# A fused transformer layer on one core: the first expert product's order, its biases, and how the last norm's rows are loaded

## The reference

```python
h = hybrid_mixer(x, ...);            x = layer_norm(ALPHA * x + h, ln1_g, ln1_b)
h = memory_cross_attention(x, ...);  x = layer_norm(ALPHA * x + h, ln2_g, ln2_b)
logits = x @ w_router + b_router     # top 4 of 32, softmax over the four
h = x @ w_gate_up[e] + b_gate_up[e]  # for each chosen expert e: 1024 -> 2048
g, u = h[:, :1024], h[:, 1024:]
g = minimum(g, 7);  u = clip(u, -7, 7)
y = ((u + 1) * g * sigmoid(1.702 * g)) @ w_down[e] + b_down[e]
x = layer_norm(ALPHA * x + sum of gate * y, ln3_g, ln3_b)
```

## Time and profile before

| | |
|---|---|
| median of 3 runs | 1207.15 us (1206.78 to 1207.22) |
| profiled execution, its own time | 1207.5 us |
| span of that profile | 1205.6 us |
| granted TensorE clock, mean | 0.995 |
| busy in the span: PE, PEld, DVE, ACT, POOL | 1148.1, 521.5, 221.0, 132.7, 49.7 us |
| DMA traffic | 446.63 MB, mean 370 GB/s |
| chain that ended last | PE 61%, DMA 35%, DVE 2% |

### The profile page before, as it was taken

How to read it: one execution, slowest core, us unless ns; L and a number is a source line. 1 busy time by engine, 2 the same in 40 slices (tenths; PEclk the granted TensorE clock), 3 DMA queues, 4 the chain that set the end, 5 groups by cost and what they waited for, 6 DMA issues and landing times.

```text
span 1205.6 us, 12958 instructions
## 1 busy us (share of the span) xinstructions
PE 1148.1 (95%) x5354; PEld 521.5 (43%) x5354; DVE 221.0 (18%) x560; ACT 132.7 (11%) x280; POOL 49.7 (4%) x56
## 2 busy tenths in 40 slices
PE   9999999999999999999999999898989899999986
PEld 7686746754434343433333443333333333333322
DVE  1233112224211111121111111111111111111114
ACT  2133102221100000001000000000000000000001
POOL 0232003010000000000000000000000000000001
PEclk9999999999999999999999999999999999999998
DMA  9953333397999999999999999999999999999995
GB/s 351 315 209 140 138 120 132 134 354 301 430 426 428 427 427 425 429 430 427 427 430 427 427 427 429 428 429 428 428 428 429 428 428 429 429 428 428 429 427 210
DMA packets 55411, 446.63 MB, mean 370 GB/s; under 512 B 10273, under 2 KB 11441, under 8 KB 30161
## 3 DMA queue, kind: packets, MB, share of 16 engines
q1 hardware_dynamic: 52912, 439.96, 87.9%
q10 hardware_dynamic: 2464, 6.18, 1.4%
HBM read 445.06 MB, written 1.07 MB: 370 GB/s over the span
## 4 chain that ended last, share of the span: by engine, by line
PE 61%; DMA 35%; DVE 2%; issue 1%; ACT 0%; SPq 0%
DMA ring<-in_w_gate_up 32%; PE bank L1673 22%; PE bank L1317 9%; PE bank L1698 9%; PE bank L1304 8%; DMA ring<-in_w_down 3%; PE bank L1557 3%; PE bank L1618 2%; PE bank L1633 1%; PE bank L1338 1%; PE bank L1744 1%; PE bank L1687 1%; PE bank L1502 1%; PE bank L1480 1%; DMA ring<-in_w_in 1%
## 5 line engine op out<-in xcount | busy, mean ns | idle before, releaser
L1673 PE MATMUL bank<-ring,PT 128*64 128x512 f32 x1848 | 409.2, 594 | 30.2 <-DMA ring<-in_w_gate_up 30.2
L1673 PEld LDWEIGHTS bank<-ring,PT 128*64 128x64 f32 x1848 | 129.7, 137 | 303.6 <-issue 242.4
L1166 DVE TENSOR_SCALAR reg_k<-bank 128x512 f32<-128x512 f32 x32 | 22.1, 692 | 455.0 <-PE bank L1673 455.0
L1304 PE MATMUL bank<-reg_bc,ring 128*128 128x256 f32 x448 | 99.7, 381 | 1.8 <-ACT reg_bc L717 1.8
L786 ACT ACTIVATE reg_v<-reg_k 128x512 f32<-128x512 f32 x30 | 18.9, 630 | 690.7 <-DVE reg_k L1166 690.7
L1698 PE MATMUL bank<-reg_q,NCt 128*64 128x512 f32 x400 | 92.5, 605 | 0.0
L1304 PEld LDWEIGHTS bank<-reg_bc,ring 128*128 128x128 f32 x448 | 84.2, 190 | 15.8 <-issue 4.8
L1698 PE MATMUL bank<-reg_bc,NCt 128*64 128x512 f32 x400 | 90.1, 592 | 0.0
L1557 PEld LDWEIGHTS bank<-L,reg_a 128*128 128x128 f32 x512 | 62.9, 196 | 24.8 <-issue 23.5
L1557 PE MATMUL bank<-L,reg_a 128*128 128x128 f32 x512 | 69.3, 288 | 1.0 <-DVE L L1080 0.7
L1197 DVE COPY reg_v<-bank 128x512 f32<-128x512 f32 x28 | 19.4, 692 | 269.0 <-PE bank L1698 269.0
(11 more groups left out here) (230 smaller groups left out, 693.1 us busy)
## 6 DMA issues: line engine op xcount, KB each, us to landing
ring<-in_w_gate_up SPq DMA_DIRECT2D x115, 2048.0 KB, 23.6
reg_bc<-in_w_down SPq DMA_DIRECT2D x26, 2048.0 KB, 20.7
reg_q<-in_w_down SPq DMA_DIRECT2D x25, 2048.0 KB, 19.2
ring<-in_w_down SPq DMA_DIRECT2D x9, 2048.0 KB, 19.0
ring<-in_w_in SPq DMA_DIRECT2D x5, 2048.0 KB, 17.7
reg_kv<-in_w_gate_up SPq DMA_DIRECT2D x5, 2048.0 KB, 18.5
reg_q<-in_w_gate_up SPq DMA_DIRECT2D x4, 2048.0 KB, 14.8
ring<-in_w_down SPq DMA_DIRECT2D x7, 1024.0 KB, 7.8
```

Of the source, the lines that this page charges most:

```text
L1166: nc.vector.tensor_scalar(gbuf, banks[0][:, :], LIMIT, None, ALU.min).then_inc(g_ready, 1)
L1304: last = mm(B(name)[:, a * T:(a + 1) * T], w[:, k, c:c + P], src[:, k, :], start=(k == 0), stop=(k == KD - 1))
L1673: last = mm(ps[half * CAP:(half + 1) * CAP, :], xgT[:, k, i * CAP:(i + 1) * CAP], w[:, j, col:col + HALF], start=False, stop=(k == KD - 1) ...
```

## The change

Five edits. (1) The first gate/up product has a function of its own, `first_gate_up`, that takes `k` in the order 1, 2, 3, 0, 4, 5, 6, 7; the lent half is thus fourth. (2) Its biases are added inside it ahead of `k` = 6, and not ahead of the rank product; in their old place stands the first tile's part of the rank. (3) Load 11 is now issued by halves like 9 and 10. (4) VectorE's order for the second tile: one copy of transposes goes to ScalarE, `gain2(0)` comes ahead, `scaled(1)` behind `rpart_copy(1)`. (5) `ln3_g` and `ln3_b` are loaded as single rows into partition 0; in the last pair TensorE multiplies a one-row matrix of ones with them (`spread_ln3`), and ScalarE copies the four results back to `x_nat`. The core of the diff:

```diff
             sp.wait_ge(opened, 2)
             load_half(NSLOT + 1, 0, ahead2_in)
-            wait_opening(1)
+            sp.wait_ge(opened, 3)
             load_half(NSLOT + 1, 1, slot_in[1])
-            for n in range(NSLOT + 2, OPEN * 2 * CH):
+            sp.wait_ge(opened, 4)
+            load_half(NSLOT + 2, 0, ahead3_in)
+            wait_opening(2)
+            load_half(NSLOT + 2, 1, slot_in[2])
+            for n in range(NSLOT + 3, OPEN * 2 * CH):
...
             copy(("rT", 1, 0), rT[:, 0:4, :], four(("rT", 1, 0)))
+            copy(("rT", 1, 1), rT[:, 4:8, :], four(("rT", 1, 1)))
             std(1, 1)
...
-            load_ln(2, ln3_g, ln3_b)
+            act.dma_start(x_nat[0:1, 0, :], ln3_g).then_inc(ln_in[2], 16)
+            act.dma_start(x_nat[0:1, 1, :], ln3_b).then_inc(ln_in[2], 16)
...
             pair(NE // 2 - 1, last=True)
+            for r in range(2):
+                act.wait_ge(ln3_rows, r + 1)
+                for half, ps in enumerate((gate_ps, up_ps)):
+                    nc.scalar.activation(x_nat[:, r, half * HALF:(half + 1) * HALF], ps[:, :], ACT.Copy).then_inc(ln3_spread, 1)
...
             variance(1, 1)
-            rT_copy(1)
-            scaled(1)
-            rpart_copy(1)
...
             dve.wait_ge(ln_in[1], 32)
+            dve.wait_ge(var_ready, TT + 2)
             gain2(0)
+            rpart_copy(1)
+            scaled(1)
             logits(1)
...
+            def rank_of_first_tile():
+                wait_bank(pe, ("rank", 1))
+                mm(B(("rank", 1))[:, 0:NE], one, M[:, 0, :], start=True, stop=False)
...
+            def first_gate_up():
+
+                pe.wait_ge(xgTa_sb, 1)
+                for n, k in enumerate((1, 2, 3, 0, 4, 5, 6, 7)):
+                    if k == 4:
+                        pe.wait_ge(xgTb_sb, 1)
+                    c, j = k // GUJ, k % GUJ
+                    if k == 0:
+                        pe.wait_ge(lent_in, 16)
+                        w = lent
+                    else:
+                        w = chunk(0, 0, c, "open")
+                    if k == 6:
+                        pe.wait_ge(bgu_in, 64)
+                        biases(0, 0, opens=False)
+                    for ps, c0 in zip((gate_ps, up_ps), (0, F)):
+                        for half in range(2):
+                            col = c0 + half * HALF
+                            last = mm(ps[half * CAP:(half + 1) * CAP, :], xgT[:, k, 0:CAP],
+                                      w[:, j, col:col + HALF], start=(n == 0), stop=(k == KD - 1), skip_group_check=True)
+                    if k in (1, 2, 3, 4):
+                        last.then_inc(opened, 1)
+                    elif k == 0:
+                        last.then_inc(chunks_used, 2)
+                    elif k == 5:
+                        last.then_inc(chunks_used, 1)
                 last.then_inc(gu_done, 1)
...
-                gate_up(0, 0, "open")
+                first_gate_up()
...
+            def spread_ln3(r):
+                if r == 0:
+                    pe.wait_ge(ln_in[2], 32)
+                    pe.wait_ge(gu_read, NE)
+                else:
+                    pe.wait_ge(ln3_spread, 2)
+                for half, ps in enumerate((gate_ps, up_ps)):
+                    last = mm(ps[:, :], one[0:1, :], x_nat[0:1, r, half * HALF:(half + 1) * HALF], start=True, stop=True)
+                last.then_inc(ln3_rows, 1)
...
-                final_down(p, 0, xy_ps, hT, lambda: transpose_h(p * 2 + 2))
+                final_down(p, 0, xy_ps, hT, second_result)
+                spread_ln3(1)
...
-            pe.wait_ge(bgu_in, 64)
-            biases(0, 0)
+            rank_of_first_tile()
             rank(1)
```

More of the change, by code:

```diff
@@ L1541, in router @@
                 fill(mm(B(name)[:, 0:NE], rsb[:, tt, :], K[:, C_STK:C_STK + NE], start=True, stop=True), name)
+            def rank_of_first_tile():
+                wait_bank(pe, ("rank", 1))
+                mm(B(("rank", 1))[:, 0:NE], one, M[:, 0, :], start=True, stop=False)
             def rank(tt):
                 name = ("rank", tt)
[L1545 to L1547 removed]
+                if tt == 0:
+                    wait_bank(pe, name)
                 pe.wait_ge(mask_ready, tt + 1)
@@ L1624, in scattered, with biases @@
                     pass
-            def biases(n, i, banks=(gate_ps, up_ps)):
+            def biases(n, i, banks=(gate_ps, up_ps), opens=True):
                 if not (type(n) is int and n < 2):
@@ L1632, in biases @@
                     rows = slice(g * 2 * NE, (g + 1) * 2 * NE)
-                    mm(ps[:, :], bsel[rows, i, :], bgu[rows, :], start=True, stop=False, skip_group_check=True)
+                    mm(ps[:, :], bsel[rows, i, :], bgu[rows, :], start=opens, stop=False, skip_group_check=True)
             def chunk(p, i, c, stage):
@@ L1659, in gate_up @@
                     pe.wait_ge(xgTa_sb, p + 1)
-                opening = stage == "open" and type(p) is int and p == 0
-                for n, k in enumerate([1, 0] + list(range(2, KD)) if opening and i == 0 else range(KD)):
+                for k in range(KD):
                     if i == 0 and k == KD // 2:
@@ L1664, in gate_up @@
                     c, j = k // GUJ, k % GUJ
-                    if n % GUJ == 0:
+                    if j == 0:
                         w = chunk(p, i, c, stage)
-                    if opening and (i, k) == (0, 0):
-                        pe.wait_ge(lent_in, 16)
-                        w = lent
                     for ps, c0 in zip(banks, (0, F)):
@@ L1674, in gate_up @@
                                       w[:, j, col:col + HALF], start=False, stop=(k == KD - 1), skip_group_check=True)
-                    if opening and (i, n) in ((0, 0), (0, 2)):
-                        last.then_inc(opened, 1)
-                    elif n % GUJ == GUJ - 1 and k < KD - 1:
+                    if j == GUJ - 1 and k < KD - 1:
                         last.then_inc(chunks_used, 1)
@@ L1680, in gate_up @@
                             behind[c]()
+                last.then_inc(gu_done, 1)
+            def first_gate_up():
[23 more added lines that the diff above has]
+                        last.then_inc(chunks_used, 1)
                 last.then_inc(gu_done, 1)
```

23 lines of the change are left out of this document (14 added, 9 removed).

## The result

The changed kernel takes **1212.95 us** (median of 5 runs, 1212.56 to 1213.87) against 1207.22 (1206.78 to 1208.47) for the kernel before: ratio 1.0047, 95% interval 1.0036 to 1.0059. It is 5.7 us slower; the prediction was 1208.0, range 1206.0 to 1209.9, so it was wrong. The profiled execution takes 1212.95 with a span of 1211.1, 5.5 more than before.

What follows compares the result with a forecast made beforehand. From about 300 us an unbroken expert-weight stream was taken to set the end, except the opening and last 25 us. Start 0, stream -2.1, spreading +2.9 gave +0.8 us: 1208.3 profiled, 1208.0 median, range 1206.0 to 1209.9.

Steps and rivals of the forecast that it cites:

- The start, 286.82, I hold fixed: Start of the first gate/up product: unchanged, net 0, between -0.2 and +0.3 us, passing one for one into the stream.
- VectorE's terms: VectorE before the first product: logits begin at about 281.05, the ranks' product at about 283.5, as before.
- The biases inside the product, 1.06, +0.9 on the mark: First gate/up product: biases ahead of its last two steps take 1.06 us; that later release costs the mark 0.9.
- the mark: Expert 2's first weight chunk: predicted to land at 309.4 against 311.5 before, a stream gain of 2.1 us.
- The halves, 2.45 apart: Opening weight loads: five 1 MB halves land 2.45 us apart, from 293.8 to 303.6.
- What stands ahead of the stream moves the whole end, one for one, and what TensorE does between is covered.: Expert-weight stream from about 300 us: its start alone sets the end, except the last 25 us, where TensorE works alone.
- The spreading, 1.74 a call: Last pair: two one-row products per call, serial, 1.74 us; first call costs 1.2, second 1.74, sum +2.9 us.
- C: Rival: stream's gain lost through slower halves or a later first product; 1210.1 us with all lost; chance 0.14.
- B: Rival: the two one-row products overlap, or the gap before the mark is absent; 1206.6 or 1207.0 us; chance 0.19.
- D: Rival: spreading hides in waits and the stream gains 3.0 us; about 1204.2 us; chance 0.05.

Runs made afterwards that it cites:

- biases back: Changed kernel with the first biases back in their old place ahead of the rank product, all else as changed: 1211.21 us, ratio 1.0024.
- rows loaded wide: Changed kernel with the last norm's rows loaded repeated over 128 partitions as before (two 512 KB loads), no spreading: 1208.92 us, ratio 1.0008.
- rows alone: Kernel before with only the norm's rows changed (two single rows loaded, spread by products in the last pair): 1211.89 us, ratio 1.0035.
- clock kept: Changed kernel plus throwaway bias products in the old place, result overwritten, the real ones still inside the first product: 1213.02 us, ratio 1.0045.
- rows hidden: Changed kernel with biases in their old place and the four one-row products moved into the last pair's gate/up products, before waits for data: 1206.97 us, ratio 0.9994.
- two row groups: Changed kernel with biases in their old place and the norm's second row in partition 64 instead of partition 0: 1208.30 us, ratio 1.0007.
- TensorE later: Kernel before with expert 1's bias products issued three times in place of once, right after the first gate/up product: 1208.03 us, ratio 1.0004.
- biases early as well: Kernel with biases in old place and one-row products hidden, plus expert 1's bias products moved to TensorE's idle time before the last gathers: 1205.88 us, ratio 0.9985.
- early biases alone: Kernel before with only expert 1's bias products moved to TensorE's idle time ahead of the last gathers: 1206.83 us, ratio 0.9991.
- longer opening: Nine-place opening for six pairs, not three, on the changed kernel, "rows hidden" and "biases early as well": 1215.40, 1208.28 and 1208.22 us.

## Why the prediction was wrong, point by point

The table sets T beside E in the profiled executions, as differences to the kernel before (305.46 and 1176.05), with the mean landing ("mean") ahead of and behind the end of the opening, and what is lost there (0.2 in the kernel before):

```
                        T     mean 340-440  mean 470 on    E      lost at 440-470
changed               +2.1       +1.1          +1.9       +2.2         1.0
biases back           +0.1       -1.8          -0.4       -1.05        1.7
rows loaded wide      +3.5       +1.7          +3.2       +3.3         1.8
rows alone            -0.1       -0.3          -0.2        0.0         0.4
clock kept            +1.2       -0.3          +0.6       +0.1         1.1
rows hidden           -0.1       -1.9          -0.6       -1.1         1.5
two row groups        +0.3       -1.5          -0.2       -0.6         1.5
TensorE later         +1.6       -0.2          +1.1       +0.3         1.5
biases early as well  -1.1       -1.7          -1.4       -1.5         0.6
early biases alone    +0.6       +1.1          +1.0       +0.7         0.0
```

(In the two runs with hidden rows TensorE waits there no longer, so their E is read from the landing of the same chunk, 1174.84 and 1174.45 against 1175.91. The last row has the late start in it.)

The two columns of the mean landing show where a stream loses: only at the opening and at its end near 450 us, and from 470 on it stays put. And they show by what rule. In all ten rows the mean landing from 470 on stands, within 0.3 us, at the later of two places: where the stream stood at 340 to 440, and T less 0.5. The 0.5 is read off these rows after the fact, so they fit the rule and do not test it. The kernel before obeys it with 0 against -0.5: there the stream's own start decides by half a microsecond, and in the changed kernel TensorE's place.

- **"The start, 286.82, I hold fixed", net 0.** Failed, and it is the first step that did. VectorE's terms were right to 0.1. What the sum left out is what the two bias products did for TensorE: in the three profiles without them in that place (changed, rows loaded wide, and the changed kernel with the longer opening) the clock fell to 0.50 to 0.59 of full in four microseconds between 284 and 290; in the eleven with them it is 1.00. Cost, +0.74 at the start and +0.19 in the first steps, 0.9 in all; in the run with the rows loaded wide more. Shown by the run with throwaway products: full clock, and first product at 286.77.
- **The biases inside the product, 1.06, +0.9 on the mark.** They cost 1.21 on TensorE. They were counted once, at the mark, and dropped behind it.
- **The halves, 2.45 apart.** Failed: of the 2.1 us of gain at the mark this term took 1.5 and something behind the fifth half the rest. In the run with throwaway products, which has the predicted start, the halves land 2.83 apart, the fifth at 305.2 and not 303.6, and the mark at 311.5 and not 309.4, which is where it was before. With the biases back the pace is 2.73 and the mark is 1.1 later than the same sum gives (309.6 and 308.5). In the changed kernel, with its late start, the mark lands at 312.7. An estimate from the 341 GB/s of the Trainium skill (DMA: Bandwidth & Descriptors, Measured) is 3.07 a half; one behind the other they took less, with `b_down` beside them.
- **"What stands ahead of the stream moves the whole end, one for one, and what TensorE does between is covered."** Failed. With the biases back the stream's mean is 1.8 earlier than before until 440 and only 0.4 from 470 on; with the stream's start untouched and T 1.6 later it is 0.2 earlier and then 1.1 later. TensorE's place decides at the end of the opening, as the rule above has it: so even the predicted gain would have been cut to what TensorE's place allows. In the changed kernel 1.1 us are lost at the opening and 0.9 more there, together 1.9. What is not settled is how the stream becomes time: E differs from the mean landing by up to 0.8 in the rows above, and the medians by as much (T 1.6 later cost 0.3, 1.0 earlier gave 1.1 and 1.0). The 428 GB/s of the windows, on which the step rested, say that the queue is not empty; they do not say by how much, and the place where it nearly is, 21.6 us without an issue at the end of the opening, stood in the trace of before and was not looked for.
- **The spreading, 1.74 a call.** The mechanism was right, on one partition the pair is serial; the size is 1.91, so +3.3 and not +2.9. Not foreseen was that such a stretch can meet the lower clock: 1.7 us in two of the five profiles that had it at 1.91 a call.
- **Rivals.** C was the nearest. Both of its ways came true, the slower halves (2.83, it had 2.9) and the late first product, the latter by the clock and not by ScalarE's copy as it names. Its 1210.1 is 2.9 short: it let the stream lose its gain and go no further, and priced the end at 2.9. B's overlap and D are refuted: 1.91, and no wait behind the second call.

Sum of the changed kernel: start and clock +0.9, biases +1.2, which put TensorE 2.1 later; the stream, its gain lost at the halves, stands with TensorE's place at 1.9 in the mean and 2.2 at E; end 3.3; 5.5 of span. The two errors that matter most, the stream (2.2 later in place of 2.1 earlier) and the end (3.3 in place of 2.9), make 4.7 of the 4.95 us between 1208.0 and 1212.95.

## What to carry to other kernels

A product that seems to stand on the path may be what keeps TensorE's clock: before taking work out of a stretch full of short waits, read how busy TensorE is left there and price the stretch at the lower clock too. Where a buffer narrows or a queue runs low, compare two places, the stream's own and the engine's that frees the buffers, and take the later. A full rate in the windows does not show that the engine behind it has slack; look for the longest gap between issues, and ask what is left in the queue at its end. Small work put at the very end costs all it takes, while the same four products in front of the last waits cost nothing (1211.2 against 1207.0), and two products that read one partition can be made to overlap by moving one row to another (1.91 to 1.06 us).

## What the runs showed of the hardware

- The granted clock fell to the lower level for a few microseconds near 285 us in 3 of 3 profiles without the two bias products, and in none of 11 with them. In the changed kernel TensorE never idled longer than 0.87 us in 278 to 287. At the end of the kernel, behind a wait of 1.33 us and a pair of one-row products, it fell in 2 of 5. It also fell near 640 us, or near 697 with the longer opening, in 7 of 14, the kernel before and the changed one among them. So the same instructions meet it in one execution and not in another, and 3 of 3 is a small count.
- A pair of products of one row by 512 columns on one partition takes 1.91 us, 0.95 each; steady products over 96 or 128 rows take 0.87 each in the earlier trace rows. So a product of one row is not cheaper. The difference may be paid once a group and not once a product: of three bias pairs in a row the first costs 1.06 and the further two 0.86 each.
- The mean of the bytes and the landing of a chunk can part by 1 us: with the longer opening the bytes came 1.2 us earlier than before to the end and the chunk at 1175.75 only 0.16 earlier.
- Three profiled executions started 1.4 to 1.7 us late by their 23rd microsecond, for no edit near it:

```profile
21.89 1.07 PE L1348 MATMUL bank<-reg_bc,wf 128*32 128x256 f32 x16
```

in the kernel before, and with the early biases alone

```profile
23.57 1.07 PE L1348 MATMUL bank<-reg_bc,wf 128*32 128x256 f32 x16
```

A difference of two single profiles below 1.7 us is therefore to be read from a common place behind it, not from the spans.
